# A transformer stack on one NeuronCore: projections wait for their split weights half by half, and later stages' tables load after the second weight block

## The reference

```python
def first_block(x, ...):
    for i in range(DEPTH):                       # 4
        a = rms_norm(h, attn_norm_g[i])
        y = diff / moba / swa (a, w_in[slot], w_out[slot], ...)
        h = h + y
        h = h + sqrelu_mlp(rms_norm(h, mlp_norm_g[i]), mlp_w_up[i], mlp_w_down[i])
    return rms_norm(h, final_norm_g)

def _layer(x, ...):                              # second stack, 2 layers
    proj = rms_norm(x) @ w_in                    # 1024 x 3104
    a, a_glu, z_conv, c_q, c_kv, k_rope, z_mla, u_sg, v_sg, z_sg = split(proj)
    y = [rms_norm(conv branch), rms_norm(latent attention), rms_norm(spatial gate)]
    return x + concat(y) @ w_out
```

## Time and profile before

| | us |
|---|---|
| median of 3 runs | 1731.67 (1728.75 to 1737.34) |
| profiled execution, device time | 1732.1 |
| its span, first to last instruction | 1730.4 |
| TensorE busy | 1560.4 (90%) |
| weight loads busy | 1343.7 (78%) |
| VectorE busy | 961.6 (56%) |
| ScalarE busy | 802.0 (46%) |
| GpSimd busy | 165.6 (10%) |
| mean granted TensorE clock | 0.947 |

### The profile page before, as it was taken

How to read it: one execution, slowest core, us unless ns; L and a number is a source line. 1 busy time by engine, 2 the same in 40 slices (tenths; PEclk the granted TensorE clock), 3 DMA queues, 4 the chain that set the end, 5 groups by cost and what they waited for, 6 DMA issues and landing times. The chain is left out here.

```text
span 1730.4 us, 21899 instructions
## 1 busy us (share of the span) xinstructions
PE 1560.4 (90%) x9045; PEld 1343.7 (78%) x9045; DVE 961.6 (56%) x1177; ACT 802.0 (46%) x1170; POOL 165.6 (10%) x165
## 2 busy tenths in 40 slices
PE   7978999999889999888999998889999787698778
PEld 5756899987679998666999886669998676587666
DVE  4554545465555455654555555445555386668754
ACT  5346543354344334433444454454444454565463
POOL 2000000000000000000000000000000295009700
PEclk8998999999999999998999999889999898899878
DMA  8312455543225554321554551224555422253220
GB/s 296 107 49 98 147 195 194 189 155 143 92 104 195 195 181 158 123 98 49 189 180 179 183 205 49 98 98 170 180 185 193 142 89 89 80 184 121 92 97 25
DMA packets 100615, 241.96 MB, mean 140 GB/s; under 512 B 2642, under 2 KB 11644, under 8 KB 100540
## 3 DMA queue, kind: packets, MB, share of 16 engines
q1 hardware_dynamic: 98848, 237.25, 38.6%
q0 software_dynamic: 1344, 3.52, 1.0%
q10 hardware_dynamic: 348, 0.13, 0.0%
HBM read 239.84 MB, written 1.05 MB: 139 GB/s over the span
## 5 line engine op out<-in xcount | busy, mean ns | idle before, releaser
L1233 DVE TENSOR_TENSOR wlo<-raw,whi 128x2048 fp32r<-128x2048 f32 (+3 forms) x240 | 509.2, 2158 | 237.6 <-ACT whi L501 237.4
L501 ACT ACTIVATE whi<-raw 128x2048 fp32r<-128x2048 f32 (+3 forms) x240 | 418.8, 1790 | 170.6 <-PE pair L862 168.6
L860 PE MATMUL pair<-whi,xhi 128*128 128x512 f32 (+2 forms) x752 | 316.2, 421 | 53.7 <-DVE wlo L1233 38.6
L861 PE MATMUL pair<-wlo,xhi 128*128 128x512 f32 (+2 forms) x752 | 302.8, 403 | 0.0
L862 PE MATMUL pair<-whi,xlo 128*128 128x512 f32 (+2 forms) x752 | 301.4, 401 | 0.0
L860 PE MATMUL pair<-xhi,whi 128*128 128x256 f32 x1024 | 291.2, 284 | 7.0 <-DVE xlo L1262 7.0
L862 PE MATMUL pair<-xhi,wlo 128*128 128x256 f32 x1024 | 290.0, 283 | 0.0
L861 PE MATMUL pair<-xlo,whi 128*128 128x256 f32 x1024 | 290.0, 283 | 0.0
L860 PEld LDWEIGHTS pair<-whi,xhi 128*128 128x128 f32 x752 | 153.1, 204 | 91.3 <-DVE wlo L1233 43.1
L860 PEld LDWEIGHTS pair<-xhi,whi 128*128 128x128 f32 x1024 | 196.5, 192 | 10.4 <-issue 6.9
L860 PE MATMUL pair<-whi,ahi 128*128 128x512 f32 x512 | 200.0, 391 | 0.0
(11 more groups left out here) (235 smaller groups left out, 1707.3 us busy)
## 6 DMA issues: line engine op xcount, KB each, us to landing
raw<-in_mlp_w_up SPq DMA_DIRECT2D x32, 2048.0 KB, 8.4
raw<-in_mlp_w_down SPq DMA_DIRECT2D x32, 2048.0 KB, 7.7
raw<-in_diff_w_in SPq DMA_DIRECT2D x11, 2048.0 KB, 7.9
raw<-in_w_in SPq DMA_DIRECT2D x10, 2048.0 KB, 7.8
raw<-in_moba_w_in SPq DMA_DIRECT2D x6, 2048.0 KB, 7.8
raw<-in_diff_w_out SPq DMA_DIRECT2D x4, 2048.0 KB, 7.8
raw<-in_w_uq SPq DMA_DIRECT2D x4, 1152.0 KB, 5.5
raw<-in_moba_w_out SPq DMA_DIRECT2D x2, 2048.0 KB, 7.8
```

Source lines behind the costliest of these rows:

```text
L501: act.activation(whi[:, s, cols], raw[:, s, cols], ACT.Copy).then_inc(*t["hi_split"].one())
L860: pe.matmul(dst, x_hi, w_hi, start=first, stop=False)
L861: pe.matmul(dst, x_hi, w_lo, start=False, stop=False)
L1233: dve.tensor_tensor(wlo[:, s, cols], raw[:, s, cols], whi[:, s, cols].bitcast(FP32), ALU.subtract)\
```

## The change

Every input projection with eight k tiles orders its units by halves of k and waits for each half of `wlo` before the unit that first needs it, and the mixers' output projections do the same with their halves; blocks with fewer k tiles, the MLP and the second stack's output projection stay. At the launch GpSimd waits for block 1's load before it issues `wsg`, `swab` and `cs2`; `swab` and `cs2` count on a semaphore of their own, for which VectorE waits before the windowed layer. The step `late` moves behind the third input block, and the making of `subg` moves with it.

```diff
--- before.py
+++ after.py
@@ -30,7 +30,8 @@
 ROUND = 1.5 * 2.0 ** 23
 TURN_PARTS = [6.28125, 0.0019350051879882812, 3.019916050e-07]
 PI_BELOW = 3.1415925
-PARAMS = 10
+PARAMS = 7
+TABLES = 3
 CW, SGW, MLAW = 256, 256, 512
 NOPE, ROPE2, QK2, V2, H2 = 64, 32, 96, 64, 8
 HALF2 = ROPE2 // 2
@@ -206,7 +207,7 @@
                      "filled9",
                      "emptied0", "emptied1", "emptied2", "emptied3", "emptied4", "emptied5", "emptied6", "emptied7", "emptied8",
                      "emptied9",
-                     "x_loaded0", "x_loaded1", "first_loaded0", "first_loaded1", "first_loaded2", "first_loaded3", "params_loaded", "gains_first", "rows_loaded", "mixing_loaded", "gains_loaded", "spread_loaded",
+                     "x_loaded0", "x_loaded1", "first_loaded0", "first_loaded1", "first_loaded2", "first_loaded3", "params_loaded", "tables_loaded", "gains_first", "rows_loaded", "mixing_loaded", "gains_loaded", "spread_loaded",
                      "pool_step", "consts_made", "mixing_masked", "dve_step", "angles_ready", "sines_ready", "params_ready",
                      "xhi_written", "bank_split", "squares_summed", "var_ready", "std_ready", "rstd_ready", "sum16_ready", "std16_ready",
                      "ahi_written", "alo_written", "roped", "heads_hi", "shift_ready", "sink_ready", "p_ready", "rstd16_ready", "h_ready",
@@ -313,7 +314,7 @@
             both = [("split", 0), ("split", 1)]
             ins = [eighths("in", b) for b in range(len(in_blocks(mixer)))]
             out0, out1 = eighths("out", 0), eighths("out", 1)
-            steps = take(ins[0], 8) + ([("late", 0)] + both + [("angles", 0)] if launch else both) + take(ins[1], 8) + [("rope", 0)]
+            steps = take(ins[0], 8) + both + ([("angles", 0)] if launch else []) + take(ins[1], 8) + [("rope", 0)]
             if mixer == "swa":
                 steps += [("split", 0)] + take(ins[2], 4) + [("heads", 0)] + head_pair(0, ins[2], 2, 0, 1)
                 steps += head_pair(1, ins[2], 2, 0) + [("rope", 1), ("features", 0)]
@@ -322,7 +323,7 @@
                 steps += [("features", 2)] + head_pair(6, out1, 2, 0, 1) + head_pair(7, out1, 2, 0)
             else:
                 fill = ins[3] + ins[4]
-                steps += both + take(ins[2], 8) + [("heads", 0)] + take(fill, 2)
+                steps += both + take(ins[2], 8) + ([("late", 0)] if launch else []) + [("heads", 0)] + take(fill, 2)
                 for h in range(4):
                     late = [("split", 0)] if h == 0 else []
                     steps += head_pair(h, fill, 3 if h < 3 else 2, 1 if h < 3 else 0, (1, None, 0, 1)[h], late)
@@ -865,7 +866,8 @@
 
 
                 units = [(tt, k) for tt in range(TT) for k in range(T)]
-                if opening or launch:
+                by_halves = T == KT
+                if by_halves:
                     units.sort(key=lambda u: u[1] // (KT // 2))
                 n = len(units)
                 some = range(n) if eighth is None else range(eighth * n // EIGHTHS, (eighth + 1) * n // EIGHTHS)
@@ -874,9 +876,10 @@
                 for u in some:
                     if launch and u in (0, n // 2):
                         pe.wait_ge(*t["bank_split"].after())
+                    if by_halves and u in (0, n // 2):
                         pe.wait_ge(*t["lo_split"].after())
                     if u == 0:
-                        if not launch:
+                        if not by_halves:
                             pe.wait_ge(*t["lo_split"].after(2))
                         free(p)
                     if opening:
@@ -918,8 +921,11 @@
                 w_hi, w_lo = slot(whi, s, 4, D), slot(wlo, s, 4, D)
                 for u in some:
                     n, tt, f = order[u]
+                    if order is BY_FEATURES and u in (0, n_units // 2):
+                        pe.wait_ge(*t["lo_split"].after())
                     if u == 0:
-                        pe.wait_ge(*t["lo_split"].after(2))
+                        if order is not BY_FEATURES:
+                            pe.wait_ge(*t["lo_split"].after(2))
                         if first:
                             free(2)
                             free(3)
@@ -1453,6 +1459,10 @@
                         t.emptied[3].n += 1
                         t.filled[1].n += 1
                         dve.wait_ge(*t.emptied[1].after())
+                        for i, init in enumerate(LAMBDA_INIT.values()):
+                            at = ROW_AT["diff_subln_g"] + i
+                            dve.tensor_scalar(subg[:, i:i + 1], colsB[:, at:at + 1], 1.0 - init, None, ALU.mult)\
+                                .then_inc(*t["params_ready"].one())
                     elif what == "angles":
                         first_parameters()
                     elif what == "rope":
@@ -1696,15 +1706,14 @@
                 dve.wait_ge(*t["sines_ready"].after(3))
                 chain(dve.tensor_tensor(neglam[:, :], lams[:, 2:4], lams[:, 0:2], ALU.subtract))
                 for n, layer in enumerate(LAMBDA_INIT):
-                    at = ROW_AT["diff_subln_g"] + n
                     dve.tensor_scalar(neglam[:, n:n + 1], neglam[:, n:n + 1], -LAMBDA_INIT[layer], None, ALU.add)\
                         .then_inc(*t["dve_step"].one())
-                    dve.tensor_scalar(subg[:, n:n + 1], colsB[:, at:at + 1], 1.0 - LAMBDA_INIT[layer], None, ALU.mult)\
-                        .then_inc(*t["params_ready"].one())
                 step()
 
             for layer, mixer in enumerate(MIXERS):
                 t.lam = layer // 3
+                if mixer == "swa":
+                    dve.wait_ge(sems["tables_loaded"], 16 * TABLES)
                 norm(gain("attn_norm_g", layer), add_mlp if layer else None, waiting=1 if layer else 0, launch=layer == 0)
                 if layer == 0:
                     split()
@@ -1832,9 +1841,6 @@
 
             pool.affine_select(out=band[:, P:2 * P], in_=band[:, P:2 * P], compare_op=ALU.is_gt, fill=NEG, base=0,
                                pattern=[[1, P]], channel_multiplier=-1).then_inc(*t["consts_made"].one())
-            for layer in range(DEPTH_2):
-                pool.dma_start(wsg[:, layer, :, :], a["sg_w_2"][layer].rearrange("g t s -> t g s"))\
-                    .then_inc(*t["mixing_loaded"].one(16))
             pool.dma_start(pos_i[:, :], a["positions"][0].rearrange("(t p) -> p t", p=P),
                            allow_slow_non_contiguous=True).then_inc(*t["params_loaded"].one(16))
             pool.dma_start(inv[:, :], a["inv_freq"].partition_broadcast(P)).then_inc(*t["params_loaded"].one(16))
@@ -1842,9 +1848,13 @@
                 pool.dma_start(lamv[:, n, :], a[key].rearrange("s d -> (s d)").partition_broadcast(P))\
                     .then_inc(*t["params_loaded"].one(16))
             pool.dma_start(sinks[:, :], a["swa_sinks"][0].partition_broadcast(P)).then_inc(*t["params_loaded"].one(16))
-            pool.dma_start(swab[:, :], a["swa_b_in"][0].partition_broadcast(P)).then_inc(*t["params_loaded"].one(16))
+            pool.wait_ge(sems["raw_loaded1"], 16)
+            for layer in range(DEPTH_2):
+                pool.dma_start(wsg[:, layer, :, :], a["sg_w_2"][layer].rearrange("g t s -> t g s"))\
+                    .then_inc(*t["mixing_loaded"].one(16))
+            pool.dma_start(swab[:, :], a["swa_b_in"][0].partition_broadcast(P)).then_inc(*t["tables_loaded"].one(16))
             for n, key in enumerate(["cos_2", "sin_2"]):
-                pool.dma_start(cs2[:, n, :, :], a[key].rearrange("(t p) n -> p t n", p=P)).then_inc(*t["params_loaded"].one(16))
+                pool.dma_start(cs2[:, n, :, :], a[key].rearrange("(t p) n -> p t n", p=P)).then_inc(*t["tables_loaded"].one(16))
 
             pool.wait_ge(*t["mixing_loaded"].now())
             pool.affine_select(out=wsg[:, :, :, :].rearrange("p l g s -> p (l g) s"),
```

## The result

| | before | after |
|---|---|---|
| median of the runs, us | 1730.21 (1725.75 to 1737.34, 4 runs) | 1705.66 (1704.93 to 1709.91, 4 runs) |
| profiled execution, us | 1732.1 | 1706.29 |
| its span, us | 1730.4 | 1704.5 |
| mean granted clock | 0.947 | 0.963 |

The ratio is 0.9869 (95% interval 0.9828 to 0.9910).

A forecast was written before the change was run, and what follows sets the result against it. TensorE's largest wait, 42.0 us for weight blocks' low halves, and low clock behind stalls were taken as the bound. Launch 5.75 plus mixers 14.55 less 3.6 returned gave 16.7 us: 1732.1 to 1715.4, range 1708 to 1724.

The forecast's parts named there:

- The launch: Launch: stall before block 1 gone (4.7 us) and low clock behind it (1.65), less 0.6 for the late step: 5.75.
- the lower bound's step: Launch: waiting for the first half alone starts block 1 at 28.85 instead of 31.15, a gain of 2.3 us.
- The half waits in a differential layer: Layers 0 and 3, last input block and first output block: 0.15 + 1.8 us and 1.4 + 2.3 us gross.
- the charge of 1.4: Either differential layer: low clock behind the replacing waits, 1.1 us for the second and 0.3 for the third.
- Layer 3: Mixer of layer 3: repeats layer 0 with clock regained, 1.4 + 2.3 us gross, 2.3 net.
- Layer 1: Mixer of layer 1: input block 2.15 us, output block 2.85, less 0.8 for the clock: 4.20 net.
- Layer 2: Mixer of layer 2: second block starts 2.25 us earlier and 1.65 of low clock behind it goes: 3.9.
- The second stack: Second stack: half waits shorten two stalls by 2.2 us, but TensorE then stands at the convolution: 0 gained.
- A: Mixers: waits mostly replaced, later steps absorb half of 14.55 us; gain 9.5, time 1722.6; chance 0.17.
- C: Launch: moved tables and late step give 3 us back, DMA in front no faster; 1722.5; chance 0.08.
- D: Whole kernel: only the launch acts, half waits come to nothing because products wait for something late; 1726.4; chance 0.05.
- B: Behind the mixers' divided stalls: low clock spreads, 20 added stretches of 1.65 us give 1744.8, slower; chance 0.04.

## Why the prediction was wrong

**The launch** (5.75): right, 6.55. The moved bytes, the 3.0 us for block 1's load, the start behind block 0 and the absent low clock each stand in a row of after; the 0.6 for the late step fit the kernel with that step moved alone. "Block 1 starts at about 26" was 25.77. Wrong was only the lower bound's step, that the half wait alone would bring block 1 to 28.85: it came to 30.70, held by the late step.

**The half waits in a differential layer**: the steps were right, and in layer 0 nothing speaks against their worth. The waits before the head transposes, the scores and the probabilities are met within 0.35 us of those forecast. Layer 0 gained 0.10 in this pair of profiles and 0.6 in the mean of all, where 0.55 was left net; neither is clear of scatter. In the profile of after a low stretch stands behind each of the replacing waits of 2.7 and 3.4 us, as the charge of 1.4 assumed; in its second profile only one does, at the later wait.

**Layer 3**: the step that failed is one that the sum did not contain: block 4's earlier start, put at nothing without a reason. As time it was absorbed, yet it made a wait of 1.31 us into one of 2.07 and brought a low stretch worth 3.0 to 3.5 us. Net, 2.3 forecast became -2.1 to -2.3 against most profiles of before (0.18 against the one on record, whose layer 3 was itself 2.5 longer).

**Layer 1** (4.2 net): 4.86. The gross terms 2.15 + 2.85 = 5.0 were right; the charge of 0.8 for the clock wasn't due, since the wait of 1.71 us lowered nothing.

**Layer 2** (3.9): 7.53 in this pair of profiles. With the half waits the mixer took 116.0 to 119.7 us and once 121.4, with whole waits 123.3 to 124.5 and once 119.8 (in the kernel with mask products before the heads, which changes nothing in this layer). What varies is the clock: the low stretches of the mixer sum to 20.5 us in before, 6.8 in after, 23.9 in after's second profile (121.4 us) and 10.2 in that exception. The 7.53 are in part luck of this pair: the middle of either group, 118.3 and 123.4, gives 5.1. The term is right for the block; the later low stretches, which come and go with the schedule, were not in it.

**The second stack** (0): this is the mistake that took the time out of the range. The sentence "It isn't touched: 0" is right for its stalls (0.1 to 0.4 us) and for the convolution as the last release, whose wait grew from 5.50 to 8.5 us. It treated the stack as a sum of waits. It holds low stretches of 20.48 us, one in the last layer, in some executions one in the layer before, at 6.4 to 6.5 us each; a shift of 0.2 to 0.4 us in when its heads start goes with their being there or not. The windows of the earlier trace rows were read around the stalls that the change removes, and not over the stages that it leaves alone; a look at the granted clock over the last layer's heads in the kernel before (0.74) would have shown up to 10 us at stake, half of 20.48. The other layer of the same trace has no such stretch in its heads and is 5.8 us faster there:

```profile
1487.73:1533.81 46.08, 38.66 (x213) 32.54 (x214) 31.70 (x51) 28.43 (x64) 0.00 (x0) 0.93 0.27 92
```

So the direction was forecast for the right reasons, and some 9 of the 23 to 26 us came from a place where none were expected. The bounds of that term should have been 0 and 13 us, and with half of it the range would have held the result.

**The rivals.** A, C and D, all with less gain, did not happen: the waits were indeed replaced (A's premise, 42.0 to 7.0 with some 20 us back), but the clock came with it. B, the clock spreading, is right as a mechanism and was wrong in sign. The rule of the Trainium skill, "TensorE: Matmul & The Clock Gate", section on a second HAM failure mode, that short idles between groups can keep the clock swinging, fits the runs in kind: a wait of 1.40 us ahead of short work stands before 20.48 us at 1.2 GHz, and with it filled the heads are 5.8 us faster. What the runs show is one long low stretch, not a clock that swings. And the kernel before already suffered from it, and the change took it away; I had weighed the rule only as a danger of the change.

**What stays open.** Why heads that start 4.79 us or more after a low stretch are followed by a long one and at 4.76 us or less are not: the cases divide without exception, but only 0.03 us lie between them, and no run varied that start alone. No run orders the units by halves and keeps the whole wait, so the part of the new order by itself is open too. And why stretches of 13.65 us came back when the waits upstream were filled, 7.0 to 7.5 us after the heads' start; the softmax waits before them were only pointed at by the trace, not tested.

## What to carry over

Read the granted clock over every stage of the kernel before, also those that the change doesn't touch: a long low stretch there is a gain or a loss that a shift of a few tenths can switch. Charge or credit the clock by the stage and not by the wait, and widen the range by it. Start a block early only where something waits for it; where the engine would only stand longer behind it, a few mask products or the old wait are worth more.

## What the hardware showed

- Behind a wait of 2.07 us between products the clock fell to 1.2 GHz in layer 3 (0.52 over the next 3.41 us); behind one of 1.61 or 1.31 at the same place it didn't, nor behind one of 1.71 in layer 1. Length alone doesn't decide: in layer 0 a wait of 2.71 us had a low stretch behind it in one profile of after and none in the other, and with the wait for the final norm filled, the clock stayed full behind a wait of 2.00 us at 1334 us.
- Waits of 1.40, 1.31 and 0.89 us among the heads' short products stood before low stretches of 20.48 and 13.65 us, in which TensorE was busy for 91% and for all of the time. The same wait of 1.40 us stands before heads without a long stretch in 20 of 28 cases. The prediction knew only waits of 1.7 us and more before low clock.
- Less low clock in all is not less time: the stretches at the low clock, summed over the trace, make 184.6 us before, 126.6 after, 136.9 in the kernel with four more mask products and 95.6 with all long waits filled, which is not faster than after.
- GpSimd's small pieces at the launch cost DMA time beyond their bytes: from 8 to 18 us, 0.28 MB in 224 packets took 27.2% of the engines, while 1.47 MB in 570 packets took 56.7%.
